# Turning the mixer's q, half of k and half of the retention operand on VectorE and through DRAM, with the heads innermost

## The reference

```python
h = rmsnorm(x); proj = h @ w_in                    # 256 x 3072
dq, dk, dv, rq, rk, rv, rg = split(proj)           # 512, 512, 512, 256, 256, 512, 512 columns
s = einsum('bhcqd,bhckd->bhcqk', q, k) * d**-0.5 + alibi   # 4 heads, 2 maps c, d = 64, causal
probs = softmax(s)[:, :, 0] - lam * softmax(s)[:, :, 1]
o_diff = head_rms(probs @ v) * g * (1 - lam_init)
scores = einsum('bnihd,bnjhd->bnhij', rq, rk) * decay      # retention, 4 heads, d = 64
o_ret = silu(rg) * head_rms(scores @ rv)                   # its recurrent form; here computed in full
x = x + concat(o_diff, o_ret) @ w_out
```

## Time and profile before

| | |
|---|---|
| median of 3 runs | 957.65 us (957.1 to 958.98) |
| the profiled execution's own time | 957.62 us |
| its span, first to last instruction | 955.8 us |
| PE busy | 945.6 us, 99% |
| DVE, ACT, POOL busy | 60%, 48%, 4% |
| granted TensorE clock | 0.998 |
| mixer of layer 0: block (1,0) to the end of (2,1) | about 204 to 228 us |
| mixer of layer 1: the same | about 674 to 698 us |

### The profile page before, as it was taken

One profiled execution on the slowest core, in us unless ns is written; L12 is line 12 of the kernel. 1 busy time (PEld: TensorE's weight loads), 2 busy tenths in 40 slices (PEclk: granted clock), 3 DMA queues, 4 the chain that ended last, 5 costly groups with the idle time before them and its releaser, 6 DMA issues.

```text
span 955.8 us, 12174 instructions
## 1 busy us (share of the span) xinstructions
PE 945.6 (99%) x4369; PEld 783.8 (82%) x4369; DVE 577.7 (60%) x712; ACT 454.3 (48%) x592; POOL 41.7 (4%) x79
## 2 busy tenths in 40 slices
PE   8999999999999999999999999999999999999997
PEld 7888888888888888888888888888888888888885
DVE  5755656566666765656466555655665767565653
ACT  7544344365564534444355434443657454434431
POOL 5030000000010000000010000000002000000000
PEclk9999999999999999999999999999999999999999
DMA  8898767534363886766639676753624748776731
GB/s 266 285 272 248 245 201 244 191 135 152 111 211 103 290 285 198 247 206 235 205 131 300 214 246 197 256 197 131 230 79 177 220 150 280 224 246 202 252 120 44
DMA packets 151626, 196.56 MB, mean 206 GB/s; under 512 B 8976, under 2 KB 119616, under 8 KB 151584
## 3 DMA queue, kind: packets, MB, share of 16 engines
q1 hardware_dynamic: 122368, 174.09, 55.0%
q10 hardware_dynamic: 28896, 21.01, 7.1%
q0 software_dynamic: 320, 0.92, 0.6%
HBM read 184.44 MB, written 11.53 MB: 205 GB/s over the span
## 4 chain that ended last, share of the span: by engine, by line
PE 97%; ACT 1%; DVE 1%; issue 0%; POOL 0%; POOLq 0%; DVEq 0%; ACTq 0%
PE gu L907 13%; PE gu L909 13%; PE gu L908 13%; PE acc L909 10%; PE acc L908 10%; PE acc L907 10%; PE tp L907 8%; PE tp L909 8%; PE tp L908 7%; PE tp L1109 1%; PE tp L925 1%; PE acc L1120 1%; PE tp L1132 1%; ACT w_hi L342 1%; PE gu L1221 1%; DVE w_lo L605 0%
## 5 line engine op out<-in xcount | busy, mean ns | idle before, releaser
L605 DVE TENSOR_TENSOR w_lo<-raw,w_hi 128x2048 fp32r<-128x2048 f32 (+1 forms) x164 | 366.1, 2236 | 108.7 <-ACT w_hi L342 108.6
L342 ACT ACTIVATE w_hi<-raw 128x2048 fp32r<-128x2048 f32 (+1 forms) x164 | 305.8, 1867 | 20.6 <-DMA raw<-in_w_up_dram 10.7
L907 PE MATMUL gu<-w_hi,xT_hi 128*128 128x512 f32 x558 | 219.7, 394 | 0.0
L909 PE MATMUL gu<-w_hi,xT_lo 128*128 128x512 f32 x558 | 217.5, 390 | 0.0
L908 PE MATMUL gu<-w_lo,xT_hi 128*128 128x512 f32 x558 | 217.2, 389 | 0.0
L907 PE MATMUL acc<-w_hi,aT_hi 128*128 128x512 f32 x384 | 150.6, 392 | 0.0
L909 PE MATMUL acc<-w_hi,aT_lo 128*128 128x512 f32 x384 | 149.7, 390 | 0.0
L908 PE MATMUL acc<-w_lo,aT_hi 128*128 128x512 f32 x384 | 149.5, 389 | 0.0
L907 PE MATMUL tp<-w_hi,xT_hi 128*128 128x512 f32 x320 | 124.7, 390 | 1.4 <-DVE w_lo L605 1.4
L908 PE MATMUL tp<-w_lo,xT_hi 128*128 128x512 f32 x320 | 124.5, 389 | 0.0
L909 PE MATMUL tp<-w_hi,xT_lo 128*128 128x512 f32 x320 | 124.5, 389 | 0.0
(11 more groups left out here) (156 smaller groups left out, 656.1 us busy)
## 6 DMA issues: line engine op xcount, KB each, us to landing
raw<-in_w_down_dram SPq DMA_DIRECT2D x88, 512.0 KB, 4.1
raw<-in_w_gate_dram SPq DMA_DIRECT2D x84, 512.0 KB, 4.1
raw<-in_w_up_dram SPq DMA_DIRECT2D x84, 512.0 KB, 5.2
raw<-in_w_in_dram SPq DMA_DIRECT2D x40, 512.0 KB, 4.7
bounce<-kT ACTq DMA_DIRECT2D x40, 256.0 KB, 4.0
qT<-bounce ACTq DMA_DIRECT2D x160, 64.0 KB, 2.1
raw<-in_w_out_dram SPq DMA_DIRECT2D x16, 512.0 KB, 3.7
raw<-in_w_in_dram SPq DMA_DIRECT2D x16, 256.0 KB, 3.0
```

The costliest lines, as they stand in the source:

```text
L342: nc.scalar.activation(w_hi[:, pos % SLOTS, 0:n], raw[:, pos % RAW, 0:n], ACT.Copy).then_inc(hi_done, 1)
L605: nc.vector.tensor_tensor(w_lo[:, pos % SLOTS, 0:n], raw[:, pos % RAW, 0:n], w_hi[:, pos % SLOTS, 0:n].bitcast(F32), ALU.subtract).then_in ...
L907: nc.tensor.matmul(out_, s_hi, m_hi, start=first, stop=False)
L909: return nc.tensor.matmul(out_, s_lo, m_hi, start=False, stop=last)
```

## The change

PE keeps the transposes of k1 and of the second token tile of `rqk` (r1). The other four sets of each layer, q0, q1, k0 and r0, go over DVE and DRAM: DVE turns the 32x32 blocks of a 128x512 tile (`to_blocks`), ACT sends the tile to DRAM (`send`, 256 KB), and fetches it back in four DMAs (`fetch`), q0 and q1 together. Runs in DRAM stay 512 B because the four heads (or four pairs of the retention) become the innermost index: `qB`, `kB` and `rB` lie as (d, token, head). So each score matmul now reads both operands with a step of four f32 (16 bytes), and the two copies that are left read PSUM with the head innermost. The turned probabilities of heads 0 and 1 go to `gate` instead of `qT` and `kT`.

```diff
+        qB, kB, rB = (t[:, :, :].rearrange("p a n -> p (a n)").rearrange("p (n i) -> p n i", i=4) for t in (qT, kT, rT))
+        turn_bounce = nc.dram_tensor("turn_bounce", (4, P, 4, P), F32).ap()
+        def turn_blocks(n):
+            t = (rv[:, 0, :], rv[:, 1, :], gate[:, 0, :], hid[:, 0:512])[n]
+            return t.rearrange("p (q n i) -> p q n i", q=4, i=4)
...
# ACT
+                def send(n, done):
+                    act.wait_ge(qkr_blocks, 4 * layer + n + 1)
+                    act.dma_start(turn_bounce[n, :, :, :].rearrange("p q n -> p (q n)"),
+                                  turn_blocks(n).rearrange("p q n i -> p (q n i)")).then_inc(done, 16)
+                def fetch(n, t, sent, landed, tiles=1):
+                    act.wait_ge(sent, 16 * tiles * (layer + 1))
+                    for q in range(4):
+                        dst = t[32 * q:32 * q + 32, 0:P * tiles, :].rearrange("c (b n) i -> c b (n i)", n=32)
+                        if tiles == 2:
+                            src = turn_bounce[n:n + 2, :, q, :].rearrange("t (b c) n -> c (t b) n", b=4)
+                        else:
+                            src = turn_bounce[n, :, q, :].rearrange("(b c) n -> c b n", b=4)
+                        act.dma_start(dst, src).then_inc(landed, 16)
...
# ACT, around r0
                     exps(tt)
+                    if tt:
+                        send(3, r_out)
                     read_proj(3, tt, rqk[:, tt, :])
...
                     prep(11 + tt, PIECE // 2)
+                    if tt == 0:
+                        fetch(3, rB, r_out, r_in)
                     read_proj(4, tt, rv[:, tt, :])
...
# DVE
+                def to_blocks(n, read, src):
+                    dve.wait_ge(proj_read, 2 * PROJ * layer + read)
+                    nc.vector.transpose(turn_blocks(n).rearrange("p q n i -> p i q n"),
+                                        src.rearrange("p (i q n) -> p i q n", i=4, q=4)).then_inc(qkr_blocks, 1)
...
-                    nc.vector.tensor_copy(dst, tp[n % 2][:, :].rearrange("p (k n) -> p k n", k=4)).then_inc(qkT_done, 1)
+                    nc.vector.tensor_copy(dst, tp[1][:, :].rearrange("p (i n) -> p n i", i=4)).then_inc(qkT_done, 1)
...
                 for tt in range(TT):
+                    if tt:
+                        to_blocks(3, 7, rqk[:, 0, :])
                     prep(9 + tt, PIECE if tt == 0 else PIECE // 2)
...
# PE
-                            ins = nc.tensor.matmul(acc[2 * (h % 2) + c][:, a:b], qT[rows, h, qt * P:(qt + 1) * P],
-                                                   kT[rows, h, 0:b - a], start=True, stop=True)
+                            ins = nc.tensor.matmul(acc[2 * (h % 2) + c][:, a:b], qB[rows, qt * P:(qt + 1) * P, h],
+                                                   kB[rows, 0:b - a, h], start=True, stop=True)
...
-                for c in (1, 2):
-                    for tt in range(TT):
-                        block_of(c, tt, lambda: qk_T(c, tt))
-                pe.wait_ge(qkT_done, 6 * layer + 4)
+                block_of(1, 0)
+                block_of(1, 1)
+                block_of(2, 0)
+                block_of(2, 1, k1_T)
+                pe.wait_ge(q_in, 64 * layer + 64)
+                pe.wait_ge(k_in, 64 * layer + 64)
+                pe.wait_ge(qkT_done, 2 * layer + 1)
                 scores(0)
                 scores(1)
...
-                for tt in range(TT):
-                    pe.wait_ge(proj_read, n_read + 7 + tt)
-                    pe.wait_ge(probsT_done, HEADS * layer + tt + 1)
-                    transposes(tp[tt], four(rqk[:, tt, :]), qkT_psum)
+                pe.wait_ge(proj_read, n_read + 8)
+                pe.wait_ge(probsT_done, HEADS * layer + 2)
+                transposes(tp[1], four(rqk[:, 1, :]), qkT_psum)
                 block_of(4, 1)
-                pe.wait_ge(qkT_done, 6 * layer + 6)
+                pe.wait_ge(r_in, 64 * layer + 64)
+                pe.wait_ge(qkT_done, 2 * layer + 2)
```

More of the change, by code:

```diff
@@ L114, in probsT @@
         def probsT(h, a, b):
-            t = (qT, kT)[h % 2]
-            return t[:, 2 * (h // 2):2 * (h // 2) + 2, :].rearrange("p a n -> p (a n)")[:, a:b]
+            t = (gate[:, 1, :], gate[:, 0, :], qT[:, 0:2, :].rearrange("p a n -> p (a n)"), kT[:, 0:2, :].rearrange("p a n -> p (a n)"))[h]
+            return t[:, a:b]
+        def turn_blocks(n):
+            t = (rv[:, 0, :], rv[:, 1, :], gate[:, 0, :], hid[:, 0:512])[n]
+            return t.rearrange("p (q n i) -> p q n i", q=4, i=4)
         def retT(h, a, b):
@@ L150, in build @@
         qkT_psum, qkT_done = sem("qkT_psum"), sem("qkT_done")
+        qkr_blocks = sem("qkr_blocks")
+        q_out, k_out, r_out, q_in, k_in, r_in = (sem(n) for n in ("q_out", "k_out", "r_out", "q_in", "k_in", "r_in"))
         scores_ready, max_done, negmax_done, exp_done, rec_steps, probs_part, probs_done = (
@@ L508, in prep @@
                     split_hi(layer, MIX0 + pos, 0, n)
+                def send(n, done):
[11 more added lines that the diff above has]
+                        act.dma_start(dst, src).then_inc(landed, 16)
                 act.wait_ge(rstd_done, TT * (3 * layer + 1) + TT)
                 prep(2)
-                for c, dst in enumerate((dq_dk[:, :, 0:512], dq_dk[:, :, 512:1024], dv[:, :, :])):
-                    for tt in range(TT):
-                        prep(2 * c + 3 + tt)
-                        read_proj(c, tt, dst[:, tt, :])
-                act.wait_ge(lam_sums, 7)
+                prep(3)
+                read_proj(0, 0, dq_dk[:, 0, 0:512])
+                prep(4)
+                send(0, q_out)
+                read_proj(0, 1, dq_dk[:, 1, 0:512])
+                prep(5)
+                send(1, q_out)
+                read_proj(1, 0, dq_dk[:, 0, 512:1024])
+                prep(6)
+                send(2, k_out)
+                act.wait_ge(lam_sums, 7)
+                fetch(0, qB, q_out, q_in, 2)
+                read_proj(1, 1, dq_dk[:, 1, 512:1024])
+                prep(7)
+                fetch(2, kB, k_out, k_in)
+                read_proj(2, 0, dv[:, 0, :])
+                prep(8)
+                read_proj(2, 1, dv[:, 1, :])
                 own = bass.ds(2 * layer, 2)
@@ L741, in prep @@
                     split_lo(layer, MIX0 + pos, 0, n)
+                def to_blocks(n, read, src):
+                    dve.wait_ge(proj_read, 2 * PROJ * layer + read)
+                    nc.vector.transpose(turn_blocks(n).rearrange("p q n i -> p i q n"),
+                                        src.rearrange("p (i q n) -> p i q n", i=4, q=4)).then_inc(qkr_blocks, 1)
                 def read_qkT(n, dst):
-                    dve.wait_ge(qkT_psum, 6 * layer + n + 1)
-                    nc.vector.tensor_copy(dst, tp[n % 2][:, :].rearrange("p (k n) -> p k n", k=4)).then_inc(qkT_done, 1)
+                    dve.wait_ge(qkT_psum, 2 * layer + n + 1)
+                    nc.vector.tensor_copy(dst, tp[1][:, :].rearrange("p (i n) -> p n i", i=4)).then_inc(qkT_done, 1)
                 def biased_max(h):
@@ L795, in mixed_lo @@
                     lo_of(dst, src[:, :].rearrange("p (k n) -> p k n", k=4), hi, mT_lo_done)
[L797 to L801, removed]
+                prep(2)
+                prep(3)
+                to_blocks(0, 1, dq_dk[:, 0, 0:512])
+                prep(4)
+                to_blocks(1, 2, dq_dk[:, 1, 0:512])
+                prep(5)
+                to_blocks(2, 3, dq_dk[:, 0, 512:1024])
+                prep(6)
+                prep(7)
+                read_qkT(0, kB[:, P:SEQ, :])
+                prep(8)
                 biased_max(0)
@@ L816, in mixer @@
                 prep(11, PIECE // 2)
-                for tt in range(TT):
-                    read_qkT(4 + tt, rT[:, :, tt * P:(tt + 1) * P])
+                read_qkT(1, rB[:, P:SEQ, :])
                 probs(2)
@@ L1144, in diff_out, with k1_T @@
                     causal(todo, pv_ready)
[L1146 to L1151, removed]
+                def k1_T():
+                    pe.wait_ge(proj_read, n_read + 4)
+                    transposes(tp[1], four(dq_dk[:, 1, 512:1024]), qkT_psum)
                 block_of(0, 0, lambda: enter_T(q, 1))
                 block_of(0, 1)
-                for c in (1, 2):
-                    for tt in range(TT):
-                        block_of(c, tt, lambda: qk_T(c, tt))
-                pe.wait_ge(qkT_done, 6 * layer + 4)
+                block_of(1, 0)
[5 more added lines that the diff above has]
+                pe.wait_ge(qkT_done, 2 * layer + 1)
                 scores(0)
@@ L1177, in mixer @@
                     rows = slice((h % 2) * QK, (h % 2 + 1) * QK)
-                    nc.tensor.matmul(acc[h][:, 0:SEQ], rT[rows, 2 + h // 2, 0:P], rT[rows, h // 2, :], start=True, stop=True)
-                    nc.tensor.matmul(acc[h][:, SEQ:384], rT[rows, 2 + h // 2, P:SEQ], rT[rows, h // 2, P:SEQ],
```

(2 more changed lines are left out.)

## The result

The changed kernel takes 970.16 us in the median of 6 runs (968.3 to 971.71), the kernel before, timed beside it, 957.66 us (956.48 to 958.98). The ratio is 1.0132, with a 95% interval of 1.0122 to 1.0142. The forecast was 954.9 us, and the range ended at 961.2: wrong in sign. The profiled execution took 970.53 us, its span is 968.7 us against 955.8, and PE's granted clock is 0.994 in the mean.

What follows compares the result with a forecast made beforehand. PE, busy in 99% of the span, was taken as the bound. From 957.6 us, 3.7 fewer for transposes, 1.0 more for waits on k's fetch and 0 for strides gave 954.9 us; range 953.2 to 961.2.

Steps and rivals of the forecast that it cites:

- The strided operands ... I take 0: Score and retention matmuls on PE: reading with a 16-byte step costs nothing, within bounds of 0 and +9.2 us in both layers.
- strides at full price: Score matmuls: both operands read at half pace, 4.61 us a layer become 9.2, total 964.1 us; chance 0.10.
- Strided weight loads alone: Score matmuls: only the stationary operand's loads slow down, 0.5 us per two heads, +3 us, total 957.9 us; chance 0.12.
- I take the middle, 3.3 us ... a wait of 0.5 us a layer: Before the first scores: k's fetch lands 3.3 us after issue, at 226.9, so PE waits 0.5 us a layer, 1.0 in all.
- the dense stretch: DMA between 24 and 96 us, share 0.90: fetches land after 4.4 us there, used as the late case for k's fetch.
- Light traffic after 224: DMA around k's fetch: idle from 224 us before the change; where traffic is light, a fetch lands after 2.1 us.
- PE is rid of 3.7 us: Mixer blocks on PE: the transposes taken away save 1.86 us a layer, 3.7 us in all.
- nothing on PE waits for the order on ACT and DVE: Mixer blocks up to the scores: sends, fetches, read-outs and splits stay hidden, by 1.5 us at (1,1) and 0.6 at (2,1).
- r0 is hidden: After block (4,0): r0's fetch lands before PE wants it, 0.40 + 5.44 us later; even a 4.4 us landing is covered.

Runs made afterwards that it cites:

- experiment 1: Kernel before, all sets still turned on PE, but score matmuls read both operands with a step of four f32, no DRAM trip; 966.87 us against 957.51.
- experiment 4: As experiment 1, but score operands read with a step of two f32 (8 bytes) in place of four; 957.95 us, one run.
- experiment 9: As experiment 2, but SP loads weight piece 9 (1 MB) only after k0 has landed; 954.45 us against 957.2.
- experiment 10: Changed kernel; q, retention at step two, k0 in 32-token blocks at step one, piece 9 held, head 0's exponentials before its split; 953.84 us against 957.2.
- experiment 2: Changed kernel with all its DRAM trips, but the scores read with a step of one; 959.38 us, ratio 1.0022.
- experiment 8: As experiment 2, but k's fetch issued later on ACT, behind the read-out of block (2,0) and the split of piece 8; 961.04 us, one run.
- experiment 3: Changed kernel, but k0 turned on PE again; q and r0 still through DRAM and strided; 964.09 us, ratio 1.0067.

## Why the prediction was wrong, by its steps

- **"The strided operands ... I take 0": this step failed.** It is the term of the sum that was mis-sized: +9.6 us (experiment 1: +9.4), the full doubling that stood as its upper bound and as the rival "strides at full price" with a chance of 0.10. The argument for nothing was that plain f32 takes its columns at 0.77 ns where f32r takes 0.44, so a slower read would keep up. The runs show no such room: the four instructions of 256 columns in the retention's scores take 1.22 us with a step of four and 0.67 with a step of two (experiments 1 and 4). The rows behind the argument told how fast PE takes columns that lie side by side, and none told how fast a strided operand can be fed; between ends of 0 and 9.2 us that did not bear 0.60 against 0.10.
- The Trainium skill's page "Advanced Engine Details and Errata", section SBUF Cachelines, gives a reason for such a price: lines of 16 bytes, a second hit on the same line needed. The runs agree with both sides of its rule: with two elements on each 16 bytes a group took 1.59 us, with one 3.06. The page has no figure for PE; the runs show one, but none shows that the lines are what slows PE.
- **"Strided weight loads alone":** they do cost (2.07 us a group), but the moving operand costs more (2.90), so this rival named the smaller half. Its size was about right, 0.57 us a group against the 0.5 taken.
- **k's fetch, "I take the middle, 3.3 us ... a wait of 0.5 us a layer": second failure.** Waits were 1.70 and 3.54 us. The issue was earlier than the text had it (219.2 to 221.2 us instead of 221.8 to 223.6), since the sends did not wait for the split ahead of them to end: q1 went out at 209.50 while the split of 208.24 was running (below). The landing was later by more: 6.6 us in the median, beyond the 4.4 of the dense stretch; layer 0 stayed within that stretch's maximum of 7.4, layer 1 with 8.4 did not. Layer 1, which the prediction counted as equal, waited twice as long. "Light traffic after 224" was read from a kernel without the added transfers; the text itself said that these would push weights into that gap, and still took half of it as light. Experiment 9 shows that the load beside it was at fault.
- **Not foreseen: the clock behind the wait**, +2.4 us. The price of a wait on PE was put at its own length.
- **Right: PE is rid of 3.7 us.** Where no wait, and no stride of four, is left, the gain shows: experiment 9 has a span of 952.3 us, and 955.8 - 3.7 = 952.1; experiment 10 is 957.2 - 953.84 = 3.4 us ahead of the kernel before.
- **Right: nothing on PE waits for the order on ACT and DVE.** The blocks follow each other as said, 33 matmuls from the first row to the second in 7.48 us, 0.2267 each, as in the earlier trace rows:

```profile
207.45 0.39 PE L959 MATMUL gu<-w_hi,xT_hi 128*128 128x512 f32 x1
...
214.93 0.39 PE L959 MATMUL gu<-w_hi,xT_hi 128*128 128x512 f32 x1
```

 ACT and DVE in this stretch, which answer to the earlier trace rows:

```profile
208.24 1.92 ACT L350 ACTIVATE w_hi<-raw 128x2048 fp32r<-128x2048 f32 x1 [0.51 <-DMA raw<-in_w_in_dram]
209.50 0.34 ACTq L520 DMA_DIRECT2D turn_bounce<-rv  x1
```

```profile
205.24 1.08 DVE L785 STREAM_TRANSPOSE rv<-wide 128x512 f32<-128x512 f32 x1
...
223.06 0.69 DVE L790 COPY kT<-tp 128x512 f32<-128x512 f32 x1 [0.66 <-PE tp L1161]
```

 A block transpose takes 1.08 us instead of the 0.9 taken, covered as said, and the copy of k1 with the head innermost takes 0.69 us as before. The block transposes stand two pieces ahead of the copies that they replace, not one as the section on the change has it; the prediction's times have them in the right place.
- **Right: r0 is hidden.** Its fetch lands after 2.0 us, where the DMA's share is down to 0.32 (244 to 246 us), and PE's chain has no wait ahead of 258.19.

## What to carry to other kernels

Before a layout puts another index innermost, count how many of the elements that PE reads in turn lie on the same 16 bytes: with two a plain f32 matmul cost almost nothing more here, with one it doubled, and most of that came from the moving operand. For a transfer that PE will wait for, read the DMA's share at that place with the transfer added, take the landing time of the dense stretch, and see whether a large load beside it can be held back for a few us. And price a wait on PE of some us above its own length, because the clock may fall behind it.

## What the runs showed of the hardware beyond what was expected

- The time of a group with a step of 16 bytes doesn't go with PE's clock: 3.06 us a group at full clock, 3.13 at half.
- After PE stood idle for 3.38 or 3.54 us it ran at 0.50 for some 6 us, and the clock had fallen before the wait was over (the mean from 704 to 706 us is 0.52, and the wait of layer 1 ended at 705.02). Waits of 1.29 to 1.64 us left the clock at 1.00 with scores of step one behind them (experiments 2 and 8); a wait of 1.70 us with strided scores behind it was followed by 0.50, while strided scores without a wait were not (1 and 3). Whether the slightly longer wait or the slow scores behind it made the difference is open.
- Four DMAs of 64 KB landed almost three times as late beside 1 MB of another queue's: 6.2 us against 2.3 (experiments 2 and 9).
